# Start addresses of the activation blocks: the first of each eight at a multiple of 128 bytes, the other seven 64 bytes past one

## What is computed

```python
def swiglu(h, w_in, w_out):                       # D_FF = 2816
    g, u = split_cols(h @ w_in, (D_FF, D_FF))
    return (jax.nn.silu(g) * u) @ w_out

# first stack, per layer: ffn1, a mixer (forgetting + differential attention, or short
# convolution + banded attention), cross-attention to a memory of 256 tokens, ffn2
x = x + 0.5 * swiglu(rms_norm(x, g[0]), ffn1_w_in[layer], ffn1_w_out[layer])
...
# second stack, per layer: ffn_pre, a mixer (retention + dilated attention, or gated
# linear attention), ffn_post; then a last norm
x = x + 0.5 * _swiglu(h, ffn_pre_w_gate[l], ffn_pre_w_up[l], ffn_pre_w_down[l])
```

## Time and profile before

| | |
|---|---|
| median of 3 runs | 2407.83 us |
| lowest, highest | 2387.07, 2414.49 us |
| the profiled execution | 2412.32 us, span 2410.5 us |
| TensorE: matmuls busy | 2297.7 us (95%), 18446 instructions |
| VectorE, ScalarE busy | 64%, 49% |
| mean granted clock of TensorE | 0.976 of full speed |

### The profile page before, as it was taken

The page is one execution under the profiler, slowest core; times in us unless marked ns, Lnnn a source line. Parts: engine busy times, 40 slices in busy tenths (PEclk is TensorE's granted clock), DMA queues, the critical chain, the costliest instruction groups (busy, mean ns, idle before and its releaser), DMA issues.

```text
span 2410.5 us, 44793 instructions
## 1 busy us (share of the span) xinstructions
PE 2297.7 (95%) x18446; PEld 2202.3 (91%) x18446; DVE 1537.8 (64%) x2216; ACT 1184.1 (49%) x1747; POOL 130.1 (5%) x146
## 2 busy tenths in 40 slices
PE   6999998889999999998999999998999999998998
PEld 6999876779999999787999999986999999988998
DVE  6756547566666766676666666667665666666664
ACT  5644434545445644445544554534544544436543
POOL 2000000100001001000100000100100000101001
PEclk9999988899999999999999999999999999999999
DMA  7555423326555557343355665642555665543653
GB/s 239 186 180 175 145 64 111 105 71 196 185 182 191 193 181 232 117 139 124 126 190 179 189 193 188 226 142 70 183 185 180 188 192 178 165 140 106 193 187 111
DMA packets 383369, 393.27 MB, mean 163 GB/s; under 512 B 6512, under 2 KB 381424, under 8 KB 383040
## 3 DMA queue, kind: packets, MB, share of 16 engines
q1 hardware_dynamic: 381248, 383.30, 49.8%
q0 software_dynamic: 1920, 7.11, 1.0%
HBM read 389.34 MB, written 1.05 MB: 162 GB/s over the span
## 4 chain that ended last, share of the span: by engine, by line
PE 88%; DVE 5%; ACT 4%; issue 1%; POOL 1%; DMA 1%; SPq 0%; POOLq 0%; ACTq 0%; DVEq 0%
PE acc L532 25%; PE acc L536 25%; PE acc L533 25%; PE wide L675 2%; PE acc L550 2%; PE acc L552 2%; PE acc L551 2%; PE wide L648 2%; ACT w_hi L816 1%; DVE w_lo L1049 1%; DVE hn_lo L1081 1%; POOL t L1433 1%; PE wide L664 1%; DMA raw<-in_ffn_w_in 1%; PE wide L603 1%
## 5 line engine op out<-in xcount | busy, mean ns | idle before, releaser
L816 ACT ACTIVATE w_hi<-raw 128x1024 fp32r<-128x1024 f32 (+1 forms) x742 | 768.5, 1040 | 967.7 <-PE acc L536 868.2
L1049 DVE TENSOR_TENSOR w_lo<-raw,w_hi 128x1024 fp32r<-128x1024 f32 (+1 forms) x742 | 889.2, 1201 | 537.6 <-ACT w_hi L816 534.7
L532 PE MATMUL acc<-hn_hi,w_hi 128*128 128x256 f32 x3536 | 855.8, 283 | 37.5 <-DMA colc<-in_cols 17.8
L533 PE MATMUL acc<-hn_lo,w_hi 128*128 128x256 f32 x3536 | 846.3, 280 | 0.0
L532 PEld LDWEIGHTS acc<-hn_hi,w_hi 128*128 128x128 f32 x3536 | 671.2, 190 | 50.9 <-DMA colc<-in_cols 17.8
L533 PEld LDWEIGHTS acc<-hn_lo,w_hi 128*128 128x128 f32 x3536 | 671.7, 190 | 0.5
L536 PE MATMUL acc<-hn_hi,w_lo 128*128 128x256 f32 x3536 | 482.1, 279 | 0.0
L536 PEld LDWEIGHTS acc<-hn_hi,w_lo 128*128 128x128 f32 x3536 | 442.1, 189 | 0.0
L532 PE MATMUL acc<-hid_hi,w_hi 128*128 128x256 f32 x1408 | 336.0, 279 | 0.0
L533 PE MATMUL acc<-hid_lo,w_hi 128*128 128x256 f32 x1408 | 336.0, 279 | 0.0
L533 PEld LDWEIGHTS acc<-hid_lo,w_hi 128*128 128x128 f32 x1408 | 265.7, 189 | 0.0
(11 more groups left out here) (199 smaller groups left out, 2042.4 us busy)
## 6 DMA issues: line engine op xcount, KB each, us to landing
raw<-in_ffn_w_in SPq DMA_DIRECT2D x88, 1024.0 KB, 5.1
raw<-in_ffn_w_out SPq DMA_DIRECT2D x32, 1024.0 KB, 5.2
raw<-in_ffn_pre_w_gate SPq DMA_DIRECT2D x22, 1024.0 KB, 5.3
raw<-in_ffn_pre_w_up SPq DMA_DIRECT2D x22, 1024.0 KB, 5.3
raw<-in_ffn_post_w_gate SPq DMA_DIRECT2D x22, 1024.0 KB, 5.3
raw<-in_ffn_post_w_up SPq DMA_DIRECT2D x22, 1024.0 KB, 5.4
raw<-in_x_w_kv SPq DMA_DIRECT2D x16, 1024.0 KB, 5.5
raw<-in_ffn_pre_w_down SPq DMA_DIRECT2D x16, 1024.0 KB, 5.1
```

The source lines that it names most:

```text
L532: nc.tensor.matmul(bank, wh[:, j, :], a_hi[:, u.k0 + j, :], start=u.first and j == 0, stop=False)
L533: nc.tensor.matmul(bank, wh[:, j, :], a_lo[:, u.k0 + j, :], start=False, stop=False)
L816: nc.scalar.activation(w_hi[:, u.slot, 0:u.nk, :], raw[:, u.raw % RING, 0:u.nk, P * u.half:P * u.half + P], ACT.Copy).then_inc(w_hi_ready, 1)
L1049: nc.vector.tensor_tensor(w_lo[:, u.slot, 0:u.nk, :], raw[:, u.raw % RING, 0:u.nk, P * u.half:P * u.half + P], w_hi[:, u.slot, 0:u.nk, :]. ...
```

## The change

The two pads go. The four tiles of normed activations become flat tiles of 8 blocks and 128 bytes more each, and a helper `rows` lays the blocks out in them: block 0 at the start of the tile (a multiple of 128 bytes), blocks 1 to 7 16 values (64 bytes) further than their plain place, so 64 past a multiple of 128. `hid_hi` and `hid_lo` become the two halves of one tile `hidden`, with blocks 0, 8 and 16 (the first of each unit) at a multiple of 128 and all others 64 past one. A new pad `before_hidden` ahead of it puts `hidden`, and with it `work`, at a multiple of 128 (64 past one before). `raw` starts at a multiple of 128 (64 past before). `w_hi`, `w_lo` and the tiles behind them keep their place relative to 128 bytes. All uses of a block change from `a[:, k, :]` to `a[k]`; no instruction, wait or DMA is added, taken away or moved.

```diff
-        before_normed = sb("before_normed", [P, 16])
-        hn_hi = sb("hn_hi", [P, KB, T], F32R)
-        hn_lo = sb("hn_lo", [P, KB, T], F32R)
-        mn_hi = sb("mn_hi", [P, KB, T], F32R)
-        mn_lo = sb("mn_lo", [P, KB, T], F32R)
+        def rows(flat, n):
+
+            at = [k * T + 32 * (k // 8) + (16 if k % 8 else 0) for k in range(n)]
+            return [flat[:, a:a + T] for a in at]
+
+        normed_hi, normed_lo, mixer_hi, mixer_lo = (
+            sb(name, [P, KB * T + 32], F32R) for name in ("normed_hi", "normed_lo", "mixer_hi", "mixer_lo"))
+        hn_hi, hn_lo, mn_hi, mn_lo = (rows(a, KB) for a in (normed_hi, normed_lo, mixer_hi, mixer_lo))
         raw = sb("raw", [P, RING, 8, CW])
-        before_weights = sb("before_weights", [P, 16])
...
-        with nc.sbuf_tensor("hid_hi", [P, HB, T], F32R) as hid_hi, nc.sbuf_tensor("hid_lo", [P, HB, T], F32R) as hid_lo:
-            pass
+        before_hidden = sb("before_hidden", [P, 16])
+        with nc.sbuf_tensor("hidden", [P, 2, HB * T + 96], F32R) as hidden:
+            hid_hi, hid_lo = rows(hidden[:, 0], HB), rows(hidden[:, 1], HB)
...
-                        nc.tensor.matmul(bank, wh[:, j, :], a_hi[:, u.k0 + j, :], start=u.first and j == 0, stop=False)
-                        nc.tensor.matmul(bank, wh[:, j, :], a_lo[:, u.k0 + j, :], start=False, stop=False)
+                        nc.tensor.matmul(bank, wh[:, j, :], a_hi[u.k0 + j], start=u.first and j == 0, stop=False)
+                        nc.tensor.matmul(bank, wh[:, j, :], a_lo[u.k0 + j], start=False, stop=False)
```

More of the change, by code:

```diff
@@ L531, in unit @@
                             pe.wait_ge(r_lo, 8 * u.need + j + 1)
-                        nc.tensor.matmul(bank, wh[:, j, :], a_hi[:, u.k0 + j, :], start=u.first and j == 0, stop=False)
-                        nc.tensor.matmul(bank, wh[:, j, :], a_lo[:, u.k0 + j, :], start=False, stop=False)
+                        nc.tensor.matmul(bank, wh[:, j, :], a_hi[u.k0 + j], start=u.first and j == 0, stop=False)
+                        nc.tensor.matmul(bank, wh[:, j, :], a_lo[u.k0 + j], start=False, stop=False)
                     pe.wait_ge(w_lo_ready, i + 1)
                     for j in range(u.nk):
-                        mm = nc.tensor.matmul(bank, wl[:, j, :], a_hi[:, u.k0 + j, :], start=False,
+                        mm = nc.tensor.matmul(bank, wl[:, j, :], a_hi[u.k0 + j], start=False,
                                               stop=u.last and j == u.nk - 1)
@@ L547, in unit @@
                     for j in range(u.nk):
-                        ah, al = a_hi[:, j, P * t:P * t + P], a_lo[:, j, P * t:P * t + P]
+                        ah, al = a_hi[j][:, P * t:P * t + P], a_lo[j][:, P * t:P * t + P]
                         wh, wl = w_hi[:, pair:pair + 2, j, :], w_lo[:, pair:pair + 2, j, :]
@@ L838, in high @@
             def high(k, gain):
-                nc.scalar.activation(hn_hi[:, k, :], x[:, k, :], ACT.Copy, scale=gains[:, gain + k:gain + k + 1])\
+                nc.scalar.activation(hn_hi[k], x[:, k, :], ACT.Copy, scale=gains[:, gain + k:gain + k + 1])\
                     .then_inc(hn_hi_ready, 1)
@@ L894, in ffn_up @@
                         act.wait_ge(hid_mul, m0 + h + 1)
-                        nc.scalar.activation(hid_hi[:, 2 * ch + h, :], hidf[:, h, :], ACT.Copy).then_inc(hid_hi_ready, 1)
+                        nc.scalar.activation(hid_hi[2 * ch + h], hidf[:, h, :], ACT.Copy).then_inc(hid_hi_ready, 1)
                     if n is not None and ch == 1:
@@ L906, in ffn_up @@
                             act.wait_ge(normed, 8 * n + k + 1)
-                            nc.scalar.activation(mn_hi[:, k, :], t1[:, k, :], ACT.Copy).then_inc(mn_hi_ready, 1)
+                            nc.scalar.activation(mn_hi[k], t1[:, k, :], ACT.Copy).then_inc(mn_hi_ready, 1)
             def cat_split(c, blocks):
@@ L922, in cat_split_blocks @@
                 for k in blocks:
-                    nc.scalar.activation(mn_hi[:, k, :], cat[:, k, :], ACT.Copy).then_inc(mn_hi_ready, 1)
+                    nc.scalar.activation(mn_hi[k], cat[:, k, :], ACT.Copy).then_inc(mn_hi_ready, 1)
             def head_norm(c, src, nb, per, gain, before, after):
@@ L1080, in low @@
                 dve.wait_ge(hn_hi_ready, 8 * gen + k + 1)
-                nc.vector.scalar_tensor_tensor(hn_lo[:, k, :], x[:, k, :], gains[:, gain + k:gain + k + 1],
-                                               hn_hi[:, k, :].bitcast(F32), ALU.mult, ALU.subtract).then_inc(hn_lo_ready, 1)
+                nc.vector.scalar_tensor_tensor(hn_lo[k], x[:, k, :], gains[:, gain + k:gain + k + 1],
+                                               hn_hi[k].bitcast(F32), ALU.mult, ALU.subtract).then_inc(hn_lo_ready, 1)
             def first_fill(gain):
@@ L1128, in cat_split @@
                     dve.wait_ge(mn_hi_ready, 8 * c.fill + k + 1)
-                    nc.vector.tensor_tensor(mn_lo[:, k, :], cat[:, k, :], mn_hi[:, k, :].bitcast(F32), ALU.subtract)\
+                    nc.vector.tensor_tensor(mn_lo[k], cat[:, k, :], mn_hi[k].bitcast(F32), ALU.subtract)\
                         .then_inc(mn_lo_ready, 1)
@@ L1174, in low_hid @@
                     dve.wait_ge(hid_mul, m0 + h + 1)
-                    nc.vector.tensor_tensor(hid_lo[:, 2 * ch + h, :], hidf[:, h, :], hid_hi[:, 2 * ch + h, :].bitcast(F32),
+                    nc.vector.tensor_tensor(hid_lo[2 * ch + h], hidf[:, h, :], hid_hi[2 * ch + h].bitcast(F32),
                                             ALU.subtract).then_inc(hid_lo_ready, 1)
@@ L1191, in mem_low @@
                             dve.wait_ge(mn_hi_ready, 8 * c.fill + k + 1)
-                            nc.vector.tensor_tensor(mn_lo[:, k, :], t1[:, k, :], mn_hi[:, k, :].bitcast(F32), ALU.subtract)\
+                            nc.vector.tensor_tensor(mn_lo[k], t1[:, k, :], mn_hi[k].bitcast(F32), ALU.subtract)\
                                 .then_inc(mn_lo_ready, 1)
```

## The result

The changed kernel takes 2449.51 us (median of 4 runs, 2447.45 to 2451.99), the kernel before 2411.16 us beside it (2387.07 to 2419.53). The ratio is 1.0176, with a 95% interval of 1.0102 to 1.0251: slower by 1.8%. The forecast of 2376 us had the wrong sign, and the range ended at 2440. The profiled execution took 2451.99 us, its span is 2450.2 us.

A forecast was written before the change was run, and what follows sets the result against it. The prediction took the kernel as bound by TensorE's stream of fp32r matmuls with a weight load each. With wide stretches gone (-43 us) and disturbances added (+7 us), 2412.3 us became 2376 us, range 2368 to 2440.

The forecast's parts named there:

- What bounds the kernel: Whole kernel: a stream of fp32r matmuls, each with its weight load; time is their number times the distance between starts.
- the two levels: Matmul starts in feed-forward stretches: a wide spacing of 117.6 ns and a narrow one of 113.2 ns, 4.4 ns apart.
- the count of 17,424: All matmuls of the stream: 3 x (3536 + 1408 + 512) of kind F and 3 x (224 + 128) of kind T.
- Block 0 at a multiple of 128: Kind F units: three matmuls each with moving block at a multiple of 128; two disturbances in each of 698 units, 1,396.
- What one disturbance costs in itself: Kind F units: +5 ns per disturbance, bounds -2 and +15; 1,396 x 5 = 7 us, ends -3 and +21 us.
- the rows at 251.6: Change of kind at 251.6: four matmuls took 0.46 us, 7 ns more than narrow; level wide before, narrow after.
- the whole gain of 43: Some 9,700 matmuls at the wide level, 4.4 ns each over narrow: 43 us gone if the stream settles narrow.
- What it does to the level: Disturbances make the level a property of the unit: 43 us gone if it settles narrow, +34 us if wide.
- Other addresses: `raw` and `work` move by 64 bytes relative to 128; slack hides slower splits, attention matmuls under 3 us, taken as 0.
- The second: Matmul stream: wide everywhere, 2412.3 + 34 = 2446 us, with up to 7 us for disturbances 2453; chance 0.25.
- The third rival: Matmul stream: a mixture as now, or nothing; 2400 to 2427 us, most likely 2410; chance 0.33.

The follow-up runs named there:

- f1: Changed kernel with tiles longer by a multiple of 256 bytes, every activation block 192 past a multiple of 256 as before: 2408.18 us, ratio 1.0019 to the kernel before.
- e1: Changed kernel with every activation block, the first of eight too, 64 bytes past a multiple of 128: 2436.41 us, ratio 1.0122 to the kernel before.
- f2: Changed kernel with distances kept modulo 256: blocks 192 past a multiple, only the first of each eight at 128: 2420.42 us, ratio 1.0065 to the kernel before.
- h1: f2 with the head block lowered only in the low tiles, one matmul in 24: 2393.84 us, ratio 0.9912 to the kernel before.
- j1: Kernel before plus a copy of low block 0 of `hn` and `hid`, 128 past a multiple of 256, read in 118 units: 2389.25 us, ratio 0.9893.
- h2: Kernel before with the high weights of 44 units in a tile apart, its first block 64 bytes further: 2416.90 us, ratio 1.0017.

## Why the prediction was wrong

*What bounds the kernel*, the two levels and their spacing, the count of 17,424: right. f1 shows both levels again, and the 39.7 us that the changed kernel lost are all in kind F, nearly all of them in its spacing.

*Block 0 at a multiple of 128: "each unit of kind F now has three matmuls" with another relation.* This step failed. It took over from the change's words that 128 bytes is the scale, and so held the other 21 matmuls for unchanged. But 14 of them (7 in blocks 8 to 15 of `hid`) now had a distance of 64 modulo 256 where they had 192, because the new tiles are 128 bytes longer and `w_hi` moved by 384; the rest kept their 192 and alternate with them. e1 has only this part and costs 1.2%; f1, which takes it back, costs nothing. In the spacing of kind F over the profiled runs, before has 115.8 ns, e1 117.1 and the changed kernel 118.2: over 16,368 matmuls some 22 us for the moved distances and some 18 us for the heads on top. The sum had nothing for the first. The sizes stood in the diff, and the trace before could not show the modulus, since all pairs of kind F had the same distance there.

*What one disturbance costs in itself:* mis-sized. Taken +5 ns each from the rows at 251.6, with +15 as the upper end; f2 shows 60 ns a unit, 40 at the head and 20 at the `w_lo` pass, 698 x 0.06 = 42 us, as much as the whole gain of 43. The reading at 251.6 was too low already: the rows are rounded to 10 ns, and by the starts the four distances there are 116, 122, 116 and 114 ns, 468 in all, 15 over the narrow level and not 7. And two changed matmuls in a row settle more slowly than that one did, over seven distances. With this price and nothing else amiss the sum would have come to 2412 - 43 + 42 = 2411 us; the other 38 us up to 2449.5 belong to the first step, and to heads which in the changed layout stand in a stream that never settles narrow.

*What it does to the level:* right in direction once the other distances are kept, shown by f2, h1 and j1: a disturbance from the moving side ended the wide level in 13 of 16 cases of h1 and j1. By h2 one from the weights' side toggles it, which I had not thought of. By itself (f2) the change as it was described makes the kernel 0.65% slower, so the forecast would have missed there too, by its price and not by its mechanism. In the changed kernel itself no stream settles narrow, so there the step did not hold.

*Other addresses* taken as nothing: right for `raw`, `work` and the splits (f1, and 1040 and 1201 ns unchanged), wrong for `w_hi` and the longer tiles, which that part did not count as moved.

*The rivals.* The second had the time, 2446 us, but not the cause: e1 without any disturbance at the head is at 1.0122. The third rival had the level as chance, which the spread of the runs bears out. The rule of the Trainium skill (page "TensorE: Matmul & The Clock Gate", Step-by-step: what each phase is for), that the two read ports are independent, would make all layouts alike; the runs differ by up to 2.5% by start addresses alone, so on this kernel the measurement decides against reading it as "no coupling". Where the coupling sits, in SBUF or in TensorE's own front, no run here tells.

What stays open is what a distance does, and why the stream holds the narrow level for long at 192 alone, when it also occurs at 64. The runs give a table, not a rule.

## What to carry to other kernels

Before calling a layout change small, write down every operand's start address before and after, modulo 256 at least, and not modulo the number in the change's name. In a stream of matmuls with a weight load each, read the spacing by stretch: if it has levels, ask what breaks them and what a break costs, and take that price from a run of at least ten matmuls. A disturbance that settles a stream need not be made in every unit: in 118 units it did as well (0.9893) as in all 698 (0.9912), with intervals that overlap.

## What was not expected of the hardware

- The spacing of 128x128 by 256 fp32r matmuls with a weight load each depends on the distance of the two operands' start addresses modulo 256 bytes: in one long stretch 116.5 to 119.8 ns at six distances, 113.2 or 117.6 at 192. More than one level occurs at 64 and 160 too, in other stretches.
- One weight tile 64 bytes off toggles the level (28 of 30 times in an unbroken stream); one moving block 64 bytes off keeps the narrow level (90 of 90 in j1) and mostly leads to it from the wide one (13 of 16 in h1 and j1), at some 20 ns each; two moving blocks in a row and one more in the same unit cost 60 ns.
